# DeltaNet triangular inversion: the updates of T and of its transpose on 32 of 64 columns

## The chip, the cores and the metric

One core of a Trainium2 chip runs the whole kernel. The time is device microseconds from the start to the end of one execution. Before the change three executions took 1493.34, 1498.42 and 1501.33 us, so the median is 1498.42 us.

## The reference

The reference is a two-layer diffusion backbone with 256 context and 256 latent tokens of width 1024. The part that matters here is the gated DeltaNet of the even layer. It has 8 heads of size 64 in two directions, and the tokens are cut into chunks of 64:

```python
lower = jnp.eye(C) + bc[..., :, None] * jnp.einsum('bnhid,bnhjd->bnhij', kc, kc) * jnp.exp(jnp.where(strict, diff, -jnp.inf))
u0 = lax.linalg.triangular_solve(lower, bc[..., None] * vc, left_side=True, lower=True, unit_diagonal=True)
wk = lax.linalg.triangular_solve(lower, (bc * jnp.exp(g))[..., None] * kc, left_side=True, lower=True, unit_diagonal=True)
```

`lower` is a unit triangular 64 x 64 matrix for each chunk, head and direction: 8 x 8 x 2 = 128 of them. The kernel inverts them and then multiplies by the inverse. All of it is fp32.

## The kernel before, in words

`stage_delta_solve` does this. The 8 chunks are taken in `NP` = 4 pairs (`ORDER`), and `l` = 0, 1 is the chunk within a pair. For one chunk the 16 matrices lie as 8 indices `r` (0 to 3 forward, 4 to 7 backward) by two halves of the partitions (0 to 63 and 64 to 127), so one tile is 128 partitions x 512 elements. The inversion doubles blocks. After `begin` (L2450), which inverts blocks of 2, each of `LV` = 5 levels joins blocks of size b = 2, 4, 8, 16 and 32. Two copies are kept: T in `Tm` (T_mat) and its transpose in `d.TT` (inv_T). One level of one chunk is

- GpSimd, `joints` (L2395): the part of the matrix that joins the blocks, by a mask, into `Om` (O_T);
- TensorE, L2252: 16 products `Om` x `Tm` of 64 x 64 by 64 columns into the bank `XY(l)`;
- ScalarE, L2350: the bank to `Xm` (X_mat);
- TensorE, L2266: 16 products `Xm` x `TT` into the bank `YT(l)`, and, except at the last level, L2268: 16 products `TT` x `Xm` into `XY(l)`, alternately with those of L2266;
- VectorE, L2521 and L2522: `Tm` minus `XY(l)`, then `TT` minus `YT(l)`, each over 128 x 512.

The order on each engine is the order of the loops. TensorE runs, for each level, the L2252 products of both chunks, then products of the modulation weights (`mods`, L425, which belong to another part of the kernel), then L2266 and L2268 of chunk 0, a filler, L2266 and L2268 of chunk 1, and a filler. The fillers prepare the next pair (`spread` L835, `gram` L2164, `keys_values` L2180, `turn` L2194) or are pieces of the recurrence of a pair that is done (`ks` L2200 and L2205, `w_` L2211, `ds` L2219 and L2222). VectorE runs the two differences of a chunk first, and then the work of the same slot: `differences`, `matrices` (L2446 and L2447), `begin` (L2454, L2455, L2457) and `values` (L2464) of the next pair, or the recurrence's `residue`, `update` and `advance`. Semaphores tie the engines together: L2252 of a level waits for the difference of L2522 of the same chunk (`up_done`, L2250), the second `spread` waits for `matrices` (`gm_done`), and the second `keys_values` waits for `values` (`vc_done`). An fp32 product appears in the trace as two weight loads and two matmuls, so the 16 products of one line and one chunk are 32 records.

Of the kernel before, what the change touches and what calls it, by code (L numbers as in the profile page):

```python
# [13 lines left out]
ALU = mybir.AluOpType  # L14
# [19 lines left out]
DNC = 64  # L34
# [1935 lines left out]
def bc(ap, shape):  # L1970
    return ap.to_broadcast(shape)
# [75 lines left out]
def stage_delta_solve(k, d, qkvT, zT, of, ob, hi, lo, row, upto):  # L2047
# [21 lines left out]
    with ExitStack() as st:  # L2069
# [4 lines left out]
        AT, Tm, Om, Xm = d.AT, d.Tm, d.Om, d.Xm  # L2074
# [6 lines left out]
        XY, YT = (lambda l: k.pb[l]), (lambda l: k.pb[2 + l])  # L2081
# [6 lines left out]
        def v8(x):  # L2088
            return x.rearrange("p (r i) -> p r i", r=8)
# [13 lines left out]
        def pair_of(s):  # L2103
            return ORDER.index(s) // 2

        def event(pi, lv, l):
            return (pi * LV + lv) * 2 + l

        def inverted(s):
            return event(pair_of(s), LV - 1, ORDER.index(s) % 2) + 1  # L2110

        def mask(lv):
            return bc(d.lev[:, lv, :, :].rearrange("p d (o i) -> p d o i", o=1), [P, 2, 4, DNC])

# [27 lines left out]
        def _(pe):  # L2142
# [98 lines left out]
            for pi in range(NP):  # L2241
                for lv in range(LV):
                    it = pi * LV + lv
                    for l in range(2):
                        e = event(pi, lv, l)
                        pe.wait_ge(om_done.sem, om_done.at(e + 1))
                        if lv == 0:
                            pe.wait_ge(t2c_done.sem, t2c_done.at(2 * pi + l + 1))
                        if e >= 2:
                            pe.wait_ge(up_done.sem, up_done.at(e - 1))  # L2250
                        for r, q in each():
                            mm = pe.matmul(XY(l)[q, r * DNC:r * DNC + DNC], Om[q, l, r, :], Tm[q, (2 * pi + l) % 4, r, :], start=True, stop=True)  # L2252
                        mm.then_inc(x_done.sem, 1)
                    for m in mods[it]:
                        mod_products(k, pe, m)
                    if it == 12:
                        mod_turn(k, pe, mod_batch(4))
                    for l in range(2):
                        e = event(pi, lv, l)
                        un = ORDER[2 * pi + l]  # L2260
                        pe.wait_ge(xc_done.sem, xc_done.at(e + 1))
                        if e < 2:
                            pe.wait_ge(kc_done.sem, kc_done.at(e + 1))
                            pe.wait_ge(vc_done.sem, vc_done.at(e + 1))
                        for r, q in each():
                            mm = pe.matmul(YT(l)[q, r * DNC:r * DNC + DNC], Xm[q, l, r, :], d.TT[q, un, r, :], start=True, stop=True)  # L2266
                            if lv < LV - 1:
                                mm = pe.matmul(XY(l)[q, r * DNC:r * DNC + DNC], d.TT[q, un, r, :], Xm[q, l, r, :], start=True, stop=True)  # L2268
                        mm.then_inc(y_done.sem, 1)
                        if (pi, lv, l) in scan:  # L2270
                            piece(*scan[pi, lv, l])
                        if pi < NP - 1:
                            j = 2 * pi + 2
                            if (lv, l) == (0, 0):
                                spread(j)
                            if (lv, l) == (0, 1):
                                gram(j)
                            if (lv, l) == (1, 1):
                                spread(j + 1)
                            if (lv, l) == (2, 0):  # L2280
                                gram(j + 1)
                            if (lv, l) == (3, 0):
                                keys_values(j)
                            if (lv, l) == (3, 1):
                                keys_values(j + 1)
                            if (lv, l) == (4, 0):
                                turn(j)
                            if (lv, l) == (4, 1):
                                turn(j + 1)
                        else:  # L2290
                            if (lv, l) == (1, 0):
                                o.pe_sums(pe)
                            if (lv, l) == (2, 1):
                                o.pe_spread(pe, 0)
                            if (lv, l) == (3, 1):
                                o.pe_spread(pe, 1)
# [130 lines left out]
        def _(dve):  # L2427
# [82 lines left out]
            for pi in range(NP):  # L2510
                more = pi < NP - 1
                for lv in range(LV):
# [3 lines left out]
                    for l in range(2):  # L2516
                        e = event(pi, lv, l)
                        un = ORDER[2 * pi + l]
                        dve.wait_ge(y_done.sem, y_done.at(e + 1))
                        if lv < LV - 1:  # L2520
                            dve.tensor_tensor(Tm[:, (2 * pi + l) % 4, :, :], Tm[:, (2 * pi + l) % 4, :, :], v8(XY(l)[:, :]), ALU.subtract)  # L2521
                        dve.tensor_tensor(d.TT[:, un, :, :], d.TT[:, un, :, :], v8(YT(l)[:, :]), ALU.subtract).then_inc(up_done.sem, 1)  # L2522
                        if (pi, lv, l) in scan:
                            piece(*scan[pi, lv, l])
                        if more:
# [1154 lines left out]
```

## Time and profile before

The profiled execution took 1496.61 us, 1.81 us less than the median. Its span from the first to the last instruction is 1494.8 us.

| | before |
|---|---|
| median of three executions | 1498.42 us |
| the profiled execution | 1496.61 us |
| its span | 1494.8 us |
| mean granted TensorE clock | 0.976 |
| TensorE busy, matmuls / weight loads | 94% / 80% |
| VectorE / ScalarE / GpSimd busy | 61% / 44% / 13% |
| HBM read | 169.26 MB |

Each matmul has a weight load (PEld) and a matmul (PE) record. The matmuls are pipelined, so the duration of one says little, and the distance between the starts of consecutive records says how fast the engine goes. "Idle before" is the time that the engine stood still just before a group, followed by what released it. "issue" is idle time for which the profile shows no wait.

### The profile page before, as it was taken

The page shows a single profiled execution, that of the slowest core. Times are in us where ns is not written, and L with a number is a line of the kernel's source. Part 1 is how long each engine was busy: PE and PEld are TensorE (multiplying, and loading weights), DVE is VectorE, ACT ScalarE, POOL GpSimd, SP SyncE. Part 2 cuts the span into 40 slices and gives each one's busy share as a digit, 9 for nine tenths or more (in the row PEclk, how much of TensorE's full clock was granted, in tenths as well). Part 3 has the DMA queues.
Part 4 walks back from the last instruction along what each step waited for, and adds up shares of the span by engine and source line. Part 5 has one row for each costly group of instructions (what it writes and reads, how often), then busy time and mean ns, then how long its engine had stood idle before and what let it go on. Part 6 is the DMA issues. An engine that isn't in the chain of part 4 may idle for free. (4 is left out here: it accounts for less than half of the span.)

```text
span 1494.8 us, 30877 instructions
## 1 busy us (share of the span) xinstructions
PE 1403.3 (94%) x13473; PEld 1190.5 (80%) x13473; DVE 917.9 (61%) x1307; ACT 654.6 (44%) x1106; POOL 200.6 (13%) x168
## 2 busy tenths in 40 slices
PE   6888999899999999999999999989999999899998
PEld 3656676778887789878888888867878679899998
DVE  4477553555464666777765215788775786788844
ACT  4235525221231245666433115444452885555534
POOL 1000000233242031556100003000001100000000
PEclk9999989799999999999999999999999999999999
DMA  9321110153325234766432232222233005466553
GB/s 343 113 62 51 57 57 14 59 171 116 116 88 143 61 111 141 225 197 197 113 103 94 87 111 92 72 85 85 83 116 113 2 29 170 113 176 191 173 167 112
DMA packets 166096, 172.29 MB, mean 115 GB/s; under 512 B 7014, under 2 KB 131786, under 8 KB 165962
## 3 DMA queue, kind: packets, MB, share of 16 engines
q1 hardware_dynamic: 155120, 148.36, 32.6%
q10 hardware_dynamic: 9754, 17.77, 3.7%
q0 software_dynamic: 1088, 4.19, 0.8%
q8 instruction: 106, 1.74, 0.5%
q14 instruction: 28, 0.23, 0.1%
HBM read 169.26 MB, written 1.05 MB: 114 GB/s over the span
## 5 line engine op out<-in xcount | busy, mean ns | idle before, releaser
L806 PE MATMUL bank<-h,w_hi 128*128 128x256 f32 (+1 forms) x952 | 327.3, 344 | 2.9 <-issue 2.9
L810 PE MATMUL bank<-h,w_lo 128*128 128x256 f32 (+1 forms) x952 | 320.0, 336 | 0.0
L809 PE MATMUL bank<-h,w_hi 128*128 128x256 f32 (+1 forms) x952 | 319.7, 336 | 0.0
L336 DVE TENSOR_TENSOR w_lo<-w_raw,w_hi 128x2048 fp32r<-128x2048 f32 (+1 forms) x91 | 209.8, 2307 | 157.5 <-ACT w_hi L296 157.3
L296 ACT ACTIVATE w_hi<-w_raw 128x2048 fp32r<-128x2048 f32 x93 | 176.2, 1897 | 143.8 <-PE bank L806 139.7
L824 DVE SCALAR_TENSOR_TENSOR acc<-bank,params,acc 128x510 f32<-128x510 f32 (+3 forms) x272 | 173.1, 645 | 89.0 <-ACT acc L1867 61.5
L806 PEld LDWEIGHTS bank<-h,w_hi 128*128 128x128 f32 x952 | 181.9, 191 | 24.1 <-issue 6.1
L809 PEld LDWEIGHTS bank<-h,w_hi 128*128 128x128 f32 x952 | 182.0, 191 | 20.7 <-issue 2.9
L810 PEld LDWEIGHTS bank<-h,w_lo 128*128 128x128 f32 x952 | 181.6, 191 | 18.8
L1867 ACT ACTIVATE acc<-bank,params 128x512 f32<-128x512 f32 (+1 forms) x88 | 48.8, 580 | 153.8 <-DVE ffn_g_lo L1888 49.8
L2395 POOL TENSOR_TENSOR O_T<-A_T,dn_consts 128x512 f32<-128x512 f32 x40 | 52.4, 1317 | 314.4 <-DVE inv_T L2457 189.2
L806 PE MATMUL bank<-h_hi,w_hi_hyb 128*128 128x512 f32 (+1 forms) x184 | 78.0, 424 | 8.4 <-DVE dn_qkv L824 3.9
L2266 PEld LDWEIGHTS bank<-inv_T,X_mat 64*64 64x64 f32 x1280 | 67.6, 133 | 20.3 <-issue 10.5
L2266 PE MATMUL bank<-inv_T,X_mat 64*64 64x64 f32 x1280 | 72.4, 220 | 3.2 <-issue 3.2
L477 POOL TENSOR_TENSOR mod_sums<-mod_sums,mod_products 128x1024 f32<-128x1024 f32 x24 | 63.3, 2636 | 83.6 <-ACT mod_products L457 82.9
L2521 DVE TENSOR_TENSOR T_mat<-T_mat,bank 128x512 f32<-128x512 f32 x32 | 21.9, 683 | 85.5 <-PE bank L2268 85.5
L810 PE MATMUL bank<-h_hi,w_lo_hyb 128*128 128x512 f32 (+1 forms) x184 | 73.6, 400 | 0.0
L809 PE MATMUL bank<-h_lo,w_hi_hyb 128*128 128x512 f32 (+1 forms) x184 | 73.6, 400 | 0.0
L2268 PE MATMUL bank<-X_mat,inv_T 64*64 64x64 f32 x1024 | 62.6, 218 | 1.7 <-issue 1.7
L2268 PEld LDWEIGHTS bank<-X_mat,inv_T 64*64 64x64 f32 x1024 | 59.6, 135 | 0.0
L806 PE MATMUL bank<-ffn_g_hi,w_hi 128*128 128x256 f32 x176 | 50.7, 288 | 2.0 <-issue 2.0
L806 PEld LDWEIGHTS bank<-h_hi,w_hi_hyb 128*128 128x128 f32 (+1 forms) x184 | 35.2, 191 | 21.5 <-issue 10.0
(435 smaller groups left out, 2980.9 us busy)
## 6 DMA issues: line engine op xcount, KB each, us to landing
w_raw<-in_ffn_up SPq DMA_DIRECT2D x86, 512.0 KB, 5.2
w_raw<-in_mod_w SPq DMA_DIRECT2D x24, 1024.0 KB, 5.3
w_raw<-in_ffn_down SPq DMA_DIRECT2D x22, 1024.0 KB, 5.0
w_raw<-in_ssm_w_in SPq DMA_DIRECT2D x20, 1024.0 KB, 5.3
mod_late<-in_mod_w ACTq DMA_DIRECT2D x16, 1024.0 KB, 5.2
w_raw<-in_hyb_w_in SPq DMA_DIRECT2D x9, 1024.0 KB, 5.3
w_raw<-in_ssm_w_out SPq DMA_DIRECT2D x8, 1024.0 KB, 4.9
mod_early<-in_mod_w SPq DMA_DIRECT2D x4, 1024.0 KB, 14.6
```

Of the source, the lines that this page charges most:

```text
L296: act.activation(hi, raw, ACT.Copy).then_inc(k.hi_done.sem, 1)
L336: dve.tensor_tensor(lo, raw, hi.bitcast(F32), ALU.subtract).then_inc(k.lo_done.sem, 1)
L477: pool.tensor_tensor(acc, acc, k.modtmp[:, (3 * i + step - 1) % 2, :, :], ALU.add).then_inc(k.mod_added.sem, 1)
L806: mm = pe.matmul(out, wh, xh, start=(start and n == 0), stop=False)
L809: pe.matmul(out, wh, xl, start=False, stop=False)
L810: mm = pe.matmul(out, wl, xh, start=False, stop=(stop and n == last))
L824: ins = dve.scalar_tensor_tensor(out=ao, in0=bo, scalar=w(j), in1=ao, op0=ALU.mult, op1=ALU.add)
L1867: act.activation(acc[:, i % 4, :], self.bank(i), ACT.Copy, scale=self.taps(i)(1)).then_inc(self.seed_done.sem, 1)
L2266: mm = pe.matmul(YT(l)[q, r * DNC:r * DNC + DNC], Xm[q, l, r, :], d.TT[q, un, r, :], start=True, stop=True)
L2268: mm = pe.matmul(XY(l)[q, r * DNC:r * DNC + DNC], d.TT[q, un, r, :], Xm[q, l, r, :], start=True, stop=True)
L2395: pool.tensor_tensor(v24(Om[:, l, :, :]), v24(at(2 * pi + l)), mask(lv + 1), ALU.mult).then_inc(om_done.sem, 1)
L2521: dve.tensor_tensor(Tm[:, (2 * pi + l) % 4, :, :], Tm[:, (2 * pi + l) % 4, :, :], v8(XY(l)[:, :]), ALU.subtract)
```

## The change

At the level that joins blocks of size b, only the half of the columns that pairs one block with the other can change: T in one half of each 2b columns, and its transpose in the other half. The backward matrices swap the halves. The change streams and subtracts only these 32 of each 64 columns. The weights (stationary operands) of the products stay 64 x 64, and the number of products, instructions, semaphores and waits is the same. The moving operand becomes a strided view with runs of b elements, each bank holds 256 packed elements in place of 512, and the differences read and write `Tm` and `TT` in runs of b elements. L2252, the copy of L2350 and the mask of L2395 are as they were.

```diff
+        def half_columns(x, lv, other):
+            b = 2 << lv
+            shift = b if other else 0
+            return bass.AP(x.tensor, x.offset + shift, [x.ap[0], [4 * DNC + b - 2 * shift, 2], [2 * b, 2 * DNC // b], [1, b]])
+
+        def half_row(x, lv, r, other):
+            b = 2 << lv
+            return x.rearrange("p (n s b) -> p n s b", s=2, b=b)[:, :, int(other != (r >= 4)), :]
+
+        def half_bank(x, lv):
+            return x[:, 0:4 * DNC].rearrange("p (d n b) -> p d n b", d=2, b=2 << lv)
@@ TensorE
                         for r, q in each():
-                            mm = pe.matmul(YT(l)[q, r * DNC:r * DNC + DNC], Xm[q, l, r, :], d.TT[q, un, r, :], start=True, stop=True)
+                            h = slice(r * DNC // 2, r * DNC // 2 + DNC // 2)
+                            mm = pe.matmul(YT(l)[q, h], Xm[q, l, r, :], half_row(d.TT[q, un, r, :], lv, r, True), start=True, stop=True)
                             if lv < LV - 1:
-                                mm = pe.matmul(XY(l)[q, r * DNC:r * DNC + DNC], d.TT[q, un, r, :], Xm[q, l, r, :], start=True, stop=True)
+                                mm = pe.matmul(XY(l)[q, h], d.TT[q, un, r, :], half_row(Xm[q, l, r, :], lv, r, False), start=True, stop=True)
@@ VectorE
                         if lv < LV - 1:
-                            dve.tensor_tensor(Tm[:, (2 * pi + l) % 4, :, :], Tm[:, (2 * pi + l) % 4, :, :], v8(XY(l)[:, :]), ALU.subtract)
-                        dve.tensor_tensor(d.TT[:, un, :, :], d.TT[:, un, :, :], v8(YT(l)[:, :]), ALU.subtract).then_inc(up_done.sem, 1)
+                            th = half_columns(Tm[:, (2 * pi + l) % 4, :, :], lv, False)
+                            dve.tensor_tensor(th, th, half_bank(XY(l), lv), ALU.subtract)
+                        ih = half_columns(d.TT[:, un, :, :], lv, True)
+                        dve.tensor_tensor(ih, ih, half_bank(YT(l), lv), ALU.subtract).then_inc(up_done.sem, 1)
```

## Rows read from the trace of the kernel before

**Rows 1.** The page: TensorE's total, and the granted clock in 40 slices.

```profile
PE 1403.3 (94%) x13473; PEld 1190.5 (80%) x13473; DVE 917.9 (61%) x1307; ACT 654.6 (44%) x1106; POOL 200.6 (13%) x168
PEclk9999989799999999999999999999999999999999
```

**Rows 2.** Stretch: length, busy PE, PEld, DVE, ACT, POOL (records), clock, DMA share, GB/s.

```profile
279.00:482.00 203.00, 189.27 (x5341) 164.83 (x5339) 100.22 (x168) 48.94 (x83) 65.71 (x60) 0.98 0.40 127
```

**Rows 3.** Groups by line, 279 to 482 us: count, busy us, mean ns, idle before.

```profile
L2266 PE MATMUL bank<-inv_T,X_mat 64*64 64x64 f32 x1280 | 72.4, 220 | 3.2 <-issue 3.2
L2268 PE MATMUL bank<-X_mat,inv_T 64*64 64x64 f32 x1024 | 62.6, 218 | 1.7 <-issue 1.7
L2522 DVE TENSOR_TENSOR inv_T<-inv_T,bank 128x512 f32<-128x512 f32 x40 | 27.2, 680 | 13.1 <-PE bank L2266 13.1
L2521 DVE TENSOR_TENSOR T_mat<-T_mat,bank 128x512 f32<-128x512 f32 x32 | 21.9, 683 | 85.5 <-PE bank L2268 85.5
```

**Rows 4.** Timeline of PE, one product block: start, us, line, operands, records.

```profile
392.49 0.34 PE L2266 MATMUL bank<-inv_T,X_mat 64*64 64x64 f32 x4
...
394.28 0.33 PE L2268 MATMUL bank<-X_mat,inv_T 64*64 64x64 f32 x4
394.40 1.15 PE L2219 MATMUL bank<-rho,kv_tok 64*64 64x64 f32 x32
```

**Rows 5.** Timeline, products with a moving operand of 4 and of 8 columns.

```profile
203.13 0.19 PEld L1025 LDWEIGHTS bank<-dn_selectors,dn_gate_rows 16*64 16x64 f32 x2
...
203.51 0.19 PEld L1025 LDWEIGHTS bank<-dn_selectors,dn_gate_rows 16*64 16x64 f32 x2
...
484.97 1.06 PE L502 MATMUL bank<-base_consts,mod_partial_sums 128*128 128x8 f32 x8
485.96 1.15 PE L2211 MATMUL bank<-rho,inv_T 64*64 64x64 f32 x32
```

**Rows 6.** Waits of PE, 279 to 482 us: total us, times, longest.

```profile
PE bank L2180 <- DVE kv_tok L2464: 2.9, 3, 1.1
PE bank L2252 <- DVE inv_T L2522: 1.1, 2, 0.5
PE bank L835 <- DVE A_T L2447: 0.8, 1, 0.8
PE bank L835 <- DVE T_mat L2643: 0.3, 1, 0.3
```

**Rows 7.** Timeline: differences of 512 and VectorE work of 256 elements; a wait of PE.

```profile
296.69 0.42 DVE L2446 TENSOR_TENSOR mq<-bank,decay 128x256 f32<-128x256 f32 x1
297.03 0.41 DVE L2447 TENSOR_TENSOR A_T<-bank,decay 128x256 f32<-128x256 f32 x1
...
308.06 0.69 DVE L2521 TENSOR_TENSOR T_mat<-T_mat,bank 128x512 f32<-128x512 f32 x1 [1.51 <-PE bank L2268]
308.67 0.68 DVE L2522 TENSOR_TENSOR inv_T<-inv_T,bank 128x512 f32<-128x512 f32 x1
...
309.50 0.30 PE L2252 MATMUL bank<-T_mat,O_T 64*64 64x64 f32 x3 [0.54 <-DVE inv_T L2522]
```

**Rows 8.** Stretches with granted clock (third figure from the end), columns as in Rows 2.

```profile
202.00:204.00 2.00, 2.00 (x47) 1.85 (x46) 0.00 (x0) 1.00 (x4) 0.00 (x0) 1.00 0.00 0
206.00:208.00 2.00, 2.00 (x34) 2.00 (x34) 0.00 (x0) 0.00 (x0) 0.00 (x0) 0.50 0.00 0
338.30:340.30 2.00, 2.00 (x44) 2.00 (x42) 0.82 (x2) 0.00 (x0) 0.00 (x0) 0.50 0.00 0
```

**Rows 9.** Timeline of PE: L2252 of both chunks at the full clock and at half.

```profile
290.31 2.08 PE L2252 MATMUL bank<-T_mat,O_T 64*64 64x64 f32 x64
...
338.83 3.31 PE L2252 MATMUL bank<-T_mat,O_T 64*64 64x64 f32 x63
```

**Rows 10.** Timeline of PE: idle before it for which no wait is shown.

```profile
337.12 0.62 PE L2211 MATMUL bank<-rho,inv_T 64*64 64x64 f32 x14 [2.15 <-issue]
...
399.30 0.21 PE L2268 MATMUL bank<-X_mat,inv_T 64*64 64x64 f32 x1 [1.70 <-issue]
```

## Prediction, made before the changed kernel ran

> **What bounds the kernel now.** I read the page first. TensorE is busy in 94% of the span and no other engine is near that [rows 1], so time is won only where TensorE's own stream gets shorter. Then I read the stretch in which the inversion runs, 279 to 482 us. In its 203.00 us TensorE is busy for 189.27 us and VectorE for 100.22 us [rows 2]. VectorE has slack on the whole, and its part of the change counts only where TensorE stands still for it. The third view is the groups by line. The products that the change touches are 1280 + 1024 = 2304 records with 72.4 + 62.6 = 135.0 us of busy time, although L2266 and L2268 alternate and overlap, and the differences are 40 + 32 = 72 instructions of about 0.68 us [rows 3]. The fourth view is the list of what TensorE waited for, because only these waits can pass a gain of VectorE on to the end.
>
> **TensorE's products.** The busy time of overlapping records is no price, so I take the distance between starts. A product block of one chunk runs from 392.49 to 394.40 us, which is 1.91 us for 64 records, or 29.8 ns each [rows 4]. The change halves the columns that stream. Whether that shortens the block depends on what sets the 29.8 ns: the 64 streamed columns or the 64 columns of weights that each record loads first. The trace has rows that keep the weights and take the stream away. L1025 and its neighbours load 64 columns of weights and stream only 4. From 203.13 to 203.51 us ten loads start (two, then eight single ones), which is 38 ns each, at the full clock [rows 5, 8]. The stream is a sixteenth of that of our products and the record is no faster. L502 loads 128 columns of weights and streams 8: eight records from 484.97 to 485.96 us, or 124 ns each [rows 5]. That is 62 ns for 64 columns, and the two halves of the partitions, which our products use in turn, make about 31 ns of it. Both rows say that the weight loads set the pace, and these stay. So I cost the halved stream at nothing, 0 us. The bounds are from the same rows. On the upper side 38 ns against 29.8 ns would be a loss, but L1025 does not alternate between halves of the partitions as our products do, so I exclude a loss from this term. On the lower side the record could become half as long, if the stream set the pace after all: 2304 x 29.8 / 2 = 34.3 us less. I take the upper end, 0, since the rows with short streams lie there.
>
> The Trainium skill speaks on the same point. Its page "TensorE: Matmul & The Clock Gate", section "Wait — 56ns, not 53.3ns?", says that the distance of two matmuls never falls below about 25 ns, however few columns stream. If that floor alone were left, my estimate by that page would be (29.8 - 25) x 2304 = 11.1 us less. The trace speaks against it here, since records with 4 columns stand 38 ns apart [rows 5].
>
> **VectorE's differences.** Two differences of 512 elements in a row start 0.61 us apart (308.06 and 308.67), and two instructions of 256 elements that also read a bank start 0.34 us apart (296.69 and 297.03) [rows 7]. So each difference gives back 0.27 us, and the pair of one chunk 0.54 us. Over 72 of them that is 19 us of VectorE, nearly all beside TensorE's work. No row of before has runs as short as 2 elements. The bounds are 0.34 us, as for long runs, and 0.61 us, as if nothing were halved. I take 0.34 us, because these rows have the same element count, type and source.
>
> What of it reaches TensorE is in the waits. TensorE waited three times for L2464 (2.9 us in all, longest 1.1), twice for L2522 (1.1 us, longest 0.5), once for L2447 (0.8 us) and once for L2643 (0.3 us) [rows 6]. In all seven the pair of differences, or one of them, stands ahead of the awaited instruction on VectorE with nothing idle between. The clearest is the wait at 309.50: L2521 starts at 308.06 when the block is done, L2522 at 308.67, and TensorE goes on at 309.50 after 0.54 us of idleness [rows 7]. The three waits for L2464 and the one for L2447 are longer than 0.54 us and give 0.54 us each, 2.2 us together. The two for L2522 have 1.1 us together and give all of it or nearly so, 1.1 us. That for L2643 gives its 0.3 us. The sum is 3.6 us less. What is late next is TensorE itself, with its weight loads. The lower bound of this gain is 0 (short runs cost like whole rows), the upper one is the sum of the four rows, 5.1 us.
>
> **TensorE's clock.** This is the term with another sign. From 202 to 208 us TensorE does nothing but records with 64 columns of weights and streams of 4 columns. It is busy in 2.00 of 2.00 us both times, but the clock is 1.00 in the first stretch and 0.50 (1.2 of 2.4 GHz) in the second [rows 8]. So the low level came although the engine was never idle, while it streamed little. The change makes 2304 records stream half as much. The inversion has a low stretch already at 338.30 to 340.30 us [rows 8], right after an idle time of 2.15 us at 337.12 [rows 10]. Another pause, 1.70 us at 399.30 us in the middle of a product block, has no low stretch behind it yet [rows 10]: around it the products of 64 columns run. With 32 columns these streams shrink too, and I expect the clock to fall there.
>
> The price comes from L2252, which runs in both states. 64 records take 2.08 us at the full clock and 63 take 3.31 us mostly at half, so 1.2 us more [rows 9]. If a block of products is caught as well, 64 records lose another 1.91 us [rows 4], which makes 3.1 us. One more low stretch then costs 1.2 to 3.1 us. I take the middle, 2.2 us, and one such stretch. The count is between none (0 us) and five, which are the four longer pauses of [rows 6] (three for L2464, one for L2447) and the one at 399.30.
>
> The Trainium skill, in "TensorE: Matmul & The Clock Gate", section "HAM oscillation — how this bites in real kernels", ties the low clock to gaps in which the engine is idle. By that rule alone this term would be 0. The trace disagrees in one place, where the clock fell with no idle time at all [rows 8].
>
> Instructions, semaphores, DMAs and their queues stay as they are, so the other terms are 0. The copy of L2350 and the mask of L2395 come no later than before.
>
> **The sum.** 0 - 3.6 + 2.2 = 1.4 us less. The profiled execution took 1496.61 us (span 1494.8 us and 1.8 us around it), so it would take 1495.2 us. It was 1.8 us faster than the median of the three runs, so my forecast for a median is 1497 us. A measurement of this kernel can tell about 0.5%, or 7.5 us, from no change, so this is no change.
>
> **The rivals.**
> *The stream sets the pace.* Then the products halve, and the sum is -34.3 - 3.6 + 2.2 = -35.7 us, or 1463 us. For it: the streamed and the loaded columns are both 64 in our records, so the rows of these records can't tell the two apart. Against it: the records with 4 and with 8 streamed columns [rows 5]. A part of the gain, half of it, would give 1480 us. Chance 0.11 for both.
> *The clock falls at all five pauses* and each time takes a block of products and the L2252 behind it along. That is 5 x 3.1 = 15.5 us, less 3.6 us, or +12 us: 1510 us, slower. For it: the low clock with a busy engine at 206 us [rows 8]. Against it: the modulation products and L2252, with full streams, stand between the blocks. It decides the sign from 3.6 us on, so from the second low stretch, and makes more than 7.5 us from the fourth. Chance 0.15.
> *The supply of instructions takes the gain.* TensorE stands still for 2.15 and 1.70 us with no wait shown [rows 10]. If it arrives earlier at such a place and only waits longer there, the 3.6 us go back: about 1499 us, or 1501 us with the clock term. Chance 0.14, within no change.
> *The change doesn't do what it says on VectorE*: short runs cost as much as whole rows. It then has 1501 us, also no change. Chance 0.05.
>
> **How the numbers follow.** My forecast itself, 1497 us, has 0.55. With the last two rivals, no change has 0.74. The first rival gives 0.11 for faster and the second 0.15 for slower. The range must leave out no more than 2 in 10: it leaves the first rival out (0.11) and the far end of the second, and takes in the bounds of the terms and the spread of the three runs (-5 to +3 us). It goes from 1488 to 1509 us.
>
> **What would show it.** If the weight loads set the pace, the product blocks in the changed trace stay at about 1.9 us for 64 records, although each matmul record is shorter. If the stream set it, they take about 1.0 us. Starts of L2521 and L2522 should stand 0.34 us apart, at all levels. The waits for L2464 should fall from 2.9 to about 1.3 us, that for L2522 from 1.1 us to almost nothing. The clock in 399 to 403 us should show 0.5 somewhere. Wrong would be: blocks clearly shorter than 1.9 us, or low stretches at three places or more that were at full clock before.

## The result, and the profile after

The changed kernel is slower by 0.4%. Its median is 1502.16 us (20 executions, 1494.77 to 1513.11), beside 1496.75 us (20 executions) for the kernel before. The ratio is 1.0038, with a 95% interval of 1.0024 to 1.0053, so the change costs 5.7 us, between 3.6 and 7.9. The forecast was 1.4 us less. Five executions of the kernels below ran with a lower granted clock and took 1568 to 1990 us, and all medians, means and ratios leave them out.

The profiled execution took 1500.1 us, 3.5 us more than that of before. First its page, the lines that answer to [rows 1]:

```profile
span 1498.3 us, 30877 instructions
PE 1407.8 (94%) x13473; PEld 1195.3 (80%) x13473; DVE 898.1 (60%) x1307; ACT 655.1 (44%) x1106; POOL 200.1 (13%) x168
PEclk9999989799999999999999999999999999999999
```

VectorE lost 20 us of busy time and TensorE gained 4.5 us. The clock in 40 slices is the same line as before and shows nothing, since a slice is 37 us long. The loss has to be looked for in shorter stretches. In the changed file L2252 is L2264, L2266 is L2279, L2268 is L2281, L2521 is L2535, L2522 is L2537, L2180 is L2192, L2464 is L2477 and L2447 is L2460. These are the groups by line of the changed kernel, 279 to 486 us, as in [rows 3]:

```profile
L2279 PE MATMUL bank<-inv_T,X_mat 64*64 64x32 f32 x1280 | 73.3, 223 | 6.1 <-issue 6.1
L2281 PE MATMUL bank<-X_mat,inv_T 64*64 64x32 f32 x1024 | 63.6, 221 | 1.5 <-issue 1.5
L2537 DVE TENSOR_TENSOR inv_T<-inv_T,bank 128x256 f32<-128x256 f32 x40 | 16.6, 415 | 20.2 <-PE bank L2279 20.1
L2535 DVE TENSOR_TENSOR T_mat<-T_mat,bank 128x256 f32<-128x256 f32 x32 | 13.4, 418 | 95.1 <-PE bank L2281 95.1
```

The products stream 32 columns and their mean record is 223 and 221 ns, as with 64 columns. Next, one product block of the changed kernel in the timeline of TensorE (start, us, line, operands, records), beside [rows 4]:

```profile
287.24 0.31 PE L2279 MATMUL bank<-inv_T,X_mat 64*64 64x32 f32 x4
...
289.01 0.30 PE L2281 MATMUL bank<-X_mat,inv_T 64*64 64x32 f32 x4
289.13 0.56 PE L2176 MATMUL bank<-dn_qkv 64*64 64x64 f32 x12
```

From 287.24 to 289.13 us it is 1.89 us for 64 records. The differences in the timeline of VectorE, beside [rows 7]:

```profile
286.28 0.42 DVE L2535 TENSOR_TENSOR T_mat<-T_mat,bank 128x256 f32<-128x256 f32 x1 [7.01 <-PE bank L2281]
286.62 0.41 DVE L2537 TENSOR_TENSOR inv_T<-inv_T,bank 128x256 f32<-128x256 f32 x1
```

They start 0.34 us apart. Of the 32 such pairs in the trace, with runs of 2 to 16 elements, 31 stand 0.33 to 0.34 us apart and one 0.28 us; before it is 0.59 to 0.61 us, and one 0.55 us. And what TensorE waited for in 279 to 482 us (total us, times, longest), beside [rows 6]:

```profile
PE bank L2279 <- issue: 6.1, 3, 3.8
PE bank L2264 <- issue: 2.0, 2, 1.2
PE bank L2281 <- issue: 1.5, 1, 1.5
PE bank L2192 <- DVE kv_tok L2477: 1.3, 2, 0.7
PE bank L835 <- issue: 0.8, 1, 0.8
PE bank L2223 <- issue: 0.5, 1, 0.5
PE bank L835 <- DVE A_T L2460: 0.3, 1, 0.3
```

The waits for VectorE fell from 5.1 us to 1.6 us, which is 3.5 us and nearly the 3.6 us that the forecast counted on. But the idle time with no wait shown is now 6.1 + 2.0 + 1.5 + 0.8 + 0.5 = 10.9 us. The same view of before has 3.2 us before L2266, 2.2 before L2211, 1.7 before L2268 and 1.6 before L2252, which is 8.7 us (8.6 us in a second profile of it). The last reading is the granted clock in stretches of 40 to 70 us (columns as in [rows 2]; the clock is the third figure from the end). First before, then after:

```profile
279.00:340.00 61.00, 56.42 (x1543) 48.73 (x1541) 27.97 (x48) 13.18 (x23) 18.21 (x17) 0.95 0.42 141
460.00:500.00 40.00, 36.52 (x835) 31.16 (x831) 18.73 (x30) 5.99 (x10) 7.66 (x8) 0.96 0.40 106
500.00:570.00 70.00, 67.29 (x583) 58.54 (x580) 46.06 (x72) 31.83 (x56) 13.12 (x18) 1.00 0.27 77
```

```profile
279.00:340.00 61.00, 57.90 (x1497) 50.16 (x1495) 20.37 (x47) 13.20 (x23) 18.05 (x16) 0.89 0.43 141
318.00:320.00 2.00, 2.00 (x43) 2.00 (x42) 1.97 (x4) 0.25 (x1) 0.00 (x0) 0.50 0.03 8
460.00:500.00 40.00, 36.16 (x825) 31.37 (x822) 13.96 (x27) 5.99 (x10) 7.82 (x9) 0.91 0.35 82
484.00:488.00 4.00, 4.00 (x69) 3.88 (x68) 2.32 (x5) 0.00 (x0) 0.00 (x0) 0.50 0.00 0
500.00:570.00 70.00, 67.82 (x602) 58.44 (x603) 44.76 (x67) 29.30 (x51) 13.15 (x18) 0.98 0.30 91
```

A stretch of length s at mean clock c holds 2 x (1 - c) x s of time at the half clock, because the clock is either 1 or 0.5. For before that is 61 x 0.10 + 40 x 0.08 + 0 = 9.3 us. For after it is 61 x 0.22 + 40 x 0.18 + 70 x 0.04 = 23.4 us. (Between 340 and 460 us the two kernels are alike.) One of the new low stretches begins in a product block:

```profile
317.01 0.25 PE L2279 MATMUL bank<-inv_T,X_mat 64*64 64x32 f32 x2 [2.00 <-issue]
...
319.42 2.79 PE L2264 MATMUL bank<-T_mat,O_T 64*64 64x64 f32 x62
```

TensorE stands still for 2.00 us, runs on, and soon after it is at 0.50; L2264 takes 2.79 us for 62 records where [rows 9] has 2.08 us for 64. So both findings of the profile are named: new idle time without a wait took the place of VectorE's, and the clock is low for longer. The experiments test both.

### The profile page after: what moved, and what is told of

Its sections match the earlier page's. It is cut to its first block and busy times, and to the rows that moved or that the text cites. A ratio compares the mean times of both kernels' runs of the same rounds, so it can differ in the third digit from the quotient of the medians.

```text
span 1498.3 us, 30877 instructions
## 1 busy us (share of the span) xinstructions
PE 1407.8 (94%) x13473; PEld 1195.3 (80%) x13473; DVE 898.1 (60%) x1307; ACT 655.1 (44%) x1106; POOL 200.1 (13%) x168
## 3 DMA queue, kind: packets, MB, share of 16 engines
q8 instruction: 106, 1.74, 0.5%
## 5 line engine op out<-in xcount | busy, mean ns | idle before, releaser
L2279 PEld LDWEIGHTS bank<-inv_T,X_mat 64*64 64x64 f32 x1280 | 67.1, 137 | 23.0 <-issue 13.4
L2279 PE MATMUL bank<-inv_T,X_mat 64*64 64x32 f32 x1280 | 73.3, 223 | 6.1 <-issue 6.1
L2535 DVE TENSOR_TENSOR T_mat<-T_mat,bank 128x256 f32<-128x256 f32 x32 | 13.4, 418 | 95.1 <-PE bank L2281 95.1
L2281 PE MATMUL bank<-X_mat,inv_T 64*64 64x32 f32 x1024 | 63.6, 221 | 1.5 <-issue 1.5
L2281 PEld LDWEIGHTS bank<-X_mat,inv_T 64*64 64x64 f32 x1024 | 58.2, 137 | 0.0
```

The costliest lines, as they stand in the source:

```text
L2279: mm = pe.matmul(YT(l)[q, h], Xm[q, l, r, :], half_row(d.TT[q, un, r, :], lv, r, True), start=True, stop=True)
L2281: mm = pe.matmul(XY(l)[q, h], d.TT[q, un, r, :], half_row(Xm[q, l, r, :], lv, r, False), start=True, stop=True)
```

## The experiments

"Half-clock time" below is 2 x (1 - mean granted clock) x span, as a mean over the executions of a kernel. It covers the whole execution. In the kernel before it is about 70 us, most of it outside the inversion.

**The two halves of the change, each alone.** The first kernel has only VectorE's half:

```diff
-                            h = slice(r * DNC // 2, r * DNC // 2 + DNC // 2)
-                            mm = pe.matmul(YT(l)[q, h], Xm[q, l, r, :], half_row(d.TT[q, un, r, :], lv, r, True), start=True, stop=True)
+                            h = slice(r * DNC, r * DNC + DNC)
+                            mm = pe.matmul(YT(l)[q, h], Xm[q, l, r, :], d.TT[q, un, r, :], start=True, stop=True)
...
-                        dve.tensor_tensor(ih, ih, half_bank(YT(l), lv), ALU.subtract).then_inc(up_done.sem, 1)
+                        dve.tensor_tensor(ih, ih, half_columns(v8(YT(l)[:, :]), lv, True), ALU.subtract).then_inc(up_done.sem, 1)
```

(The product into `XY(l)` and the difference of `Tm` likewise.)

> The products stream all 64 columns again and only the differences take 32 columns (they read the wanted half of each bank in place). If the loss of the change comes from TensorE's clock because less is streamed (my theory), this version keeps the 3.6 us that the shorter differences give back and none of the loss: about 1493 us, ratio to before 0.997 to 0.998, and stretches at half clock within 300 to 500 us only where the kernel before has them. If the loss comes from the strided short runs of the differences, or only from the moved order of events, it is still there: ratio 1.003 or more.

Measured: 1497.3 us (12 executions) beside 1495.8, a ratio of 1.0003 (0.9991 to 1.0015). Half-clock time 70.3 us, before 69.8 us. So there is no clock loss, and the expected gain of 3.6 us did not come either. What TensorE waited for in this kernel, 279 to 482 us:

```profile
PE bank L2279 <- issue: 6.2, 2, 3.7
PE bank L2264 <- issue: 2.1, 2, 1.3
PE bank L2281 <- issue: 1.7, 1, 1.7
PE bank L2192 <- DVE kv_tok L2477: 1.3, 2, 0.8
PE bank L2223 <- issue: 1.2, 1, 1.2
PE bank L835 <- DVE A_T L2460: 0.3, 1, 0.3
```

The waits for VectorE are 1.6 us here too, 3.5 us below before. The idle time without a wait is 11.2 us in place of 8.7. It gives most of the gain back. The second kernel has only TensorE's half. VectorE gets its old work back, and some more, as an extra instruction beside each difference:

```diff
                             th = half_columns(Tm[:, (2 * pi + l) % 4, :, :], lv, False)
+                            tr = half_columns(Tm[:, (2 * pi + l) % 4, :, :], lv, True)
+                            dve.tensor_tensor(tr, tr, tr, ALU.max)
                             dve.tensor_tensor(th, th, half_bank(XY(l), lv), ALU.subtract)
```

(The same for `d.TT`.)

> The products stream 32 columns, as in the change, but VectorE does as much as before: each difference of 256 elements has a second instruction of 256 elements beside it (a maximum of the other half with itself, which changes nothing). Clock theory: the loss without the gain, so before plus 5.4 plus 3.6 us, about 1506 us, ratio 1.006, and low-clock stretches as in the changed kernel. Rival (the differences cause the loss): no loss, ratio 1.000. Rival (the stream sets the pace and something else hides it): below 1.000.

Measured: 1503.1 us (6 executions), ratio 1.0044 (1.0027 to 1.0061), which is +6.6 us. Half-clock time 90.1 us. The loss is there without VectorE's gain, so it comes with the short streams. As a price of the streams alone the figure is rough: VectorE is busy for 108.2 us in 279 to 482 us here and for 100.2 us before, and TensorE waits for it for 9.5 us instead of 5.1. A cleaner pair follows with the fourth kernel.

**A dose.** The third kernel streams 8 columns in the same products:

```diff
-                            h = slice(r * DNC // 2, r * DNC // 2 + DNC // 2)
-                            mm = pe.matmul(YT(l)[q, h], Xm[q, l, r, :], half_row(d.TT[q, un, r, :], lv, r, True), start=True, stop=True)
+                            h = slice(r * DNC // 2, r * DNC // 2 + 8)
+                            mm = pe.matmul(YT(l)[q, h], Xm[q, l, r, :], d.TT[q, un, r, 0:8], start=True, stop=True)
```

> The changed kernel with products that stream 8 columns instead of 32; so most of the updates is left out and the output is not the reference's. TensorE does the same number of products with the same weight loads and a quarter of the streaming. Clock theory: much slower, at least 10 us over the changed kernel, up to 50 us, with half-clock stretches in most rounds of the inversion; where the clock is full the blocks of 64 records stay at 1.9 us. If the stream sets the pace of the blocks it is faster than before by 30 us or more. If streaming matters for neither, it equals the changed kernel within 0.3%.

Measured: 1513.87 us (3 executions), ratio 1.0124 (1.0102 to 1.0146), which is +18.5 us. Half-clock time 131.1 us. The fourth kernel is the change once more, beside these three.

> The changed kernel once more, for a second profile on the same chip as the three others. Clock theory: ratio 1.004, and in this profile again more half-clock time between 300 and 500 us than in before (6.8 us there), at places that follow a pause beside the products of 32 columns, but not the same ones. If the low stretches of the first profile were chance, this one has as many as before and the cause is open.

Measured: 1502.57 us (7 executions), ratio 1.0041 (1.0025 to 1.0056); half-clock time 94.3 us. Against the first kernel the differences are the same size and only the products stream 32 columns instead of 64 (and pack their results): by the means that is 5.8 us more, give or take 2.4. In 300 to 500 us the clock is 0.93 in this profile and 0.98 before. The stretches show where the low clock lies. First streams of 64 columns with half differences, then the change again, then streams of 8:

```profile
279.00:340.00 61.00, 57.00 (x1550) 48.80 (x1547) 21.10 (x46) 13.79 (x24) 19.60 (x18) 0.96 0.43 141
```

```profile
279.00:340.00 61.00, 58.41 (x1461) 51.03 (x1459) 19.76 (x45) 13.30 (x23) 18.13 (x17) 0.86 0.42 140
460.00:500.00 40.00, 36.16 (x744) 30.61 (x742) 11.85 (x22) 7.35 (x13) 9.51 (x10) 0.83 0.35 81
```

```profile
400.00:460.00 60.00, 56.04 (x1582) 52.07 (x1578) 28.12 (x56) 15.53 (x26) 17.47 (x17) 0.91 0.27 91
```

With 8 columns even 400 to 460 us, where the kernels with streams of 64 and of 32 columns above stand at 1.00, falls to 0.91. The four kernels ran beside each other, so their means can be set against their half-clock time:

| products stream | mean time | half-clock time | us per us of half clock, against the first |
|---|---|---|---|
| 64 columns (first kernel) | 1496.7 us | 70.3 us | |
| 32, full work on VectorE (second) | 1502.9 us | 90.1 us | 6.2 / 19.8 = 0.31 |
| 32, the change (fourth) | 1502.5 us | 94.3 us | 5.8 / 24.0 = 0.24 |
| 8 columns (third) | 1514.8 us | 131.1 us | 18.1 / 60.8 = 0.30 |

The fewer columns stream, the longer the clock is low, and each such microsecond costs 0.24 to 0.31 us. It can't cost more than 0.5, as work at half speed for 1 us is 0.5 us of work left over, and part of the time TensorE idles. The 20 executions of the changed kernel, which all do the same work, say the same without any comparison of kernels. The one with the least half-clock time (71.7 us) took 1494.77 us, the one with the most (114.9 us) took 1513.11 us, and a line through all 20 rises by 0.39 us per us (correlation 0.95). The four with less than 75 us took 1494.8 to 1497.1 us, as does the kernel before (median 1496.75 us).

**What sets the pace of a product block.** Two kernels take the kernel before and cut the weights to 32 columns, one with streams of 64 columns, one with 32:

```diff
-                            mm = pe.matmul(YT(l)[q, r * DNC:r * DNC + DNC], Xm[q, l, r, :], d.TT[q, un, r, :], start=True, stop=True)
+                            few = slice(q.start, q.start + DNC // 2)
+                            mm = pe.matmul(YT(l)[few, r * DNC:r * DNC + 64], Xm[q, l, r, 0:DNC // 2], d.TT[q, un, r, 0:64], start=True, stop=True)
```

> The kernel before with products of the updates that load 32 columns of weights instead of 64 and stream 64; the other half of each result is left out, so the output is not the reference's. If the weight loads alone set the pace, as predicted, a block of 64 records falls from 1.9 to about 1.0 us and the kernel is faster by up to 33 us, unless instructions can't be supplied so fast. If the stream holds the pace just as much (64 columns each, side by side), the block stays at 1.9 us and the time is that of before, ratio 1.000.

> As the run before, but the products stream 32 columns too; again part of the work is left out. Both limits of the block are halved. If loads and streams are the two limits, a block of 64 records takes about 1.0 us and the kernel could save 33 us less what the clock takes. If the supply of instructions is the limit behind them, TensorE's idle time without a shown wait, about 9 us in before, grows by tens of us and at most 10 us are saved.

Weights of 32 and streams of 64 columns: 1494.95 us, ratio 0.9993 (0.9976 to 1.001). Both at 32: 1488.14 us, ratio 0.9949 (0.9923 to 0.9975). The starts of groups of 4 records, first the one, then the other, then the kernel with streams of 8 columns and full weights:

```profile
300.76 0.30 PE L2267 MATMUL bank<-inv_T,X_mat 64*32 64x64 f32 x4
...
300.99 0.30 PE L2267 MATMUL bank<-inv_T,X_mat 64*32 64x64 f32 x4
```

```profile
292.04 0.25 PE L2267 MATMUL bank<-inv_T,X_mat 64*32 64x32 f32 x4
...
293.43 0.25 PE L2267 MATMUL bank<-inv_T,X_mat 64*32 64x32 f32 x4
```

```profile
284.85 0.28 PE L2279 MATMUL bank<-inv_T,X_mat 64*64 64x8 f32 x4
...
285.08 0.28 PE L2279 MATMUL bank<-inv_T,X_mat 64*64 64x8 f32 x4
```

Weights 32, stream 64 is 0.23 us for 8 records, or 29 ns each. Weights 64, stream 8 is also 0.23 us for 8. Both at 32 is 1.39 us from 292.04 to 293.43 for 88 records, or 15.8 ns each. So the loads and the stream are two limits of equal height, and to remove one leaves the other. The Trainium skill's "TensorE: Matmul & The Clock Gate", section "Wait — 56ns, not 53.3ns?", states a floor of about 25 ns between the starts of two matmuls. The trace shows 15.8 ns here, in a stream of records that alternates between the two halves of the partitions. Within one half that is 31.6 ns on the mean.

With both at 32, the product blocks should save 2304 x (29.8 - 15.8) ns = 32 us, and the execution gains 7.6 us. TensorE's idle time without a wait grew from 8.7 to 16.3 us there, and the waits for VectorE from 5.1 to 6.4 us. Half-clock time went from 68.3 to 80.7 us. At 0.3 us per us that is an estimated 4 us. With the longer idle times and the 7.6 us gained, about 20 of the 32 us are accounted for; where the rest went is open. The forecast that the idle time would grow by tens of us was too high.

**The differences as small as can be.** If VectorE were still in the way, differences of next to nothing would help. This is the first kernel with differences of 16 elements:

```diff
-                        dve.tensor_tensor(ih, ih, half_columns(v8(YT(l)[:, :]), lv, True), ALU.subtract).then_inc(up_done.sem, 1)
+                        dve.tensor_tensor(d.TT[:, un, 0, 0:16], d.TT[:, un, 0, 0:16], YT(l)[:, 0:16], ALU.subtract).then_inc(up_done.sem, 1)
```

> The kernel of the first experiment (streams of 64) with each difference cut to 16 elements, so the updates are left out nearly whole. VectorE's share of every wait of TensorE is gone: about 0.55 us more for each of the waits that were left. If gains of VectorE reach the end, this is 3 us or more faster than before, ratio 0.998 or less. If the supply of instructions takes them, as I now think, the time stays within 1.5 us of before, and TensorE's pauses before its records number 2614, 3122, 4013, 4776, 6174 and 6937 (counted from its first) add up to more than the 12.5 us of the first experiment.

Measured: 1495.51 us, ratio 0.9992 (0.9977 to 1.0007). What TensorE waited for, 279 to 482 us:

```profile
PE bank L2279 <- issue: 6.3, 3, 4.1
PE bank L2264 <- issue: 2.6, 3, 1.4
PE bank L2223 <- issue: 2.3, 1, 2.3
PE bank L2281 <- issue: 1.4, 1, 1.4
PE bank L2192 <- DVE kv_tok L2477: 0.7, 1, 0.7
```

VectorE holds TensorE up for 0.7 us in all, and there is no gain. The idle time without a wait is 12.6 us. VectorE's waits and this idle time together are 13.8 us before, 12.8 with half differences and 13.3 with tiny ones. So most of what VectorE no longer holds up comes back as idle time without a wait. The kernel before was profiled once more beside it.

> The kernel before once more, for a second profile. If the pauses without a shown wait are the supply of instructions, they stand before the same records of TensorE as in the first profile (3122, 4776, 6174, 6937) whatever the time of day in the run; there is none, or a short one, before 2614 and 4013, where TensorE has just waited for VectorE. Low-clock stretches between 300 and 500 us: about 7 us in all.

One execution took 1498.1 us. The four pauses stand before the same records as in the first profile. Two more came, before 4013 (0.9 us) and 4394 (1.1 us), so which of the places show a pause varies from one execution to the next, and where they are does not.

**Where the pauses without a wait come from.** Every pause has one of a few places in the count of TensorE's 13473 matmul records. I list the number of records before each pause of over 0.6 us for which no wait stands (in brackets the us from start to start), from 309 to 482 us:

| kernel | pauses |
|---|---|
| before | 3122 (2.4), 4776 (1.9), 6174 (1.5), 6937 (3.4) |
| before again | 3122 (1.3), 4013 (0.9), 4394 (1.1), 4776 (1.7), 6174 (1.3), 6937 (3.7) |
| after | 2614 (2.2), 3122 (0.8), 4013 (1.1), 4394 (1.1), 4776 (1.7), 6174 (1.4), 6937 (4.1) |
| differences alone | 2614 (2.7), 3122 (1.4), 4013 (1.1), 4776 (2.0), 6174 (1.5), 6937 (3.9) |
| tiny differences | 2486 (0.8), 2614 (1.9), 3122 (2.5), 4013 (1.6), 4776 (1.6), 6174 (1.2), 6937 (4.3) |

The distances are multiples of 127, give or take a record or two: 3122 - 2614 = 508 = 4 x 127, 4013 - 3122 = 891 = 7 x 127, 4776 - 4394 = 382 = 3 x 127, 6174 - 4776 = 1398 = 11 x 127, 6937 - 6174 = 763 = 6 x 127. The page of before has 106 packets of 16.4 KB on the DMA queue "q8 instruction" (1.74 MB). In the kernel before, one of them is under way in 334 to 338 us, where TensorE pauses with no wait, and in the kernel with half differences one is in 311 to 316 us:

```profile
q8 instruction: 1, 0.02, 1.8%
```

```profile
q8 instruction: 1, 0.02, 1.2%
```

The pause in the timeline of the latter:

```profile
315.15 0.37 PE L2279 MATMUL bank<-inv_T,X_mat 64*64 64x64 f32 x2 [2.52 <-issue]
```

The page after has the same 106 packets. 13473 records by 106 packets are 127.1 records a packet, the step of the table. That reads as an engine whose next packet of instructions is late, and the times of the packets in the traces bear it out. I take the two profiles of before, the two of the change, and those of the kernels with half differences, with streams alone, with tiny differences and with the 32 added records below. In 279 to 486 us they have 47 pauses of TensorE of over 0.4 us with no wait shown, and every one ends 1.23 to 1.56 us after a packet of this queue has ended. In before the packets end at 335.88, 397.84, 444.98 and 478.86 us, and TensorE goes on at 337.12, 399.30, 446.40 and 480.29 us. The 33 pauses with a wait end at any distance from a packet (0.04 to 6.81 us), and none of them in that range. It can be tested by an edit, too: insert records and see whether the pauses move with the program or stay at their count.

```diff
             turn(1)
+            for r, q in each():
+                pe.matmul(O[q, r * DNC:r * DNC + DNC], d.TT[q, ORDER[0], r, :], k.ident[q, q], start=True, stop=True)
             for pi in range(NP):
```

> The kernel before with 16 more products (32 records of TensorE, 0.9 us) at the start of the inversion, into a bank that nobody reads then. It shows what the pauses without a shown wait hang on. Supply of instructions: they stay at the same count of records from the start of the program (3122, 4776, 6174, 6937), so 32 records earlier in the work. Anything tied to the work (a missing record of a wait, a bank, a buffer): they come 32 records later in the count (3154, 4808, 6206, 6969). The waits for VectorE (2129, 2433, 2633, 3729, 3937, 5545 in before) move by 32 in either case.

These are 32 records more. Five of the six pauses with a wait moved by exactly 32: 2129, 2433, 2633, 3937 and 5545 became 2161, 2465, 2665, 3969 and 5577. The sixth, 3729, should stand at 3761. There is none; a pause of the other kind stands two records ahead of it, at 3759, with no wait shown, and covers it. (30 of the 64 records of L2254, L2252 before, come ahead of it and 34 behind it, so it lies two records before the second chunk.)

```profile
357.32 1.27 PE L2254 MATMUL bank<-T_mat,O_T 64*64 64x64 f32 x34 [0.88 <-issue]
```

It ends 1.27 us after a packet, and 3759 is 4013 - 2 x 127. The other pauses without a wait stand at 2486, 3249, 4267, 4904, 6174, 6937 and 7065, and none at 3154, 4808, 6206 or 6969. Two of the four expected numbers stayed (6174 and 6937). The other two are gone, and pauses stand one step further on: 3249 is 3122 + 127, 4904 is 4776 + 128. So the pauses belong to the count of instructions and not to a piece of work. Their lengths change, too: 0.8 us at 3249, where the profile of before has 2.4 us at 3122. The one execution took 1493.95 us with more work in it. One execution against a spread of several microseconds says nothing on the time.

**Can the clock be kept up with wider streams?** In [rows 8] it falls at 206 us, behind products that stream 4 columns (L1025 and its neighbours). One kernel repeats their moving operand 16 times, so they stream 64 columns, and takes them in an order that alternates between the two halves of the output's partitions (before, five products in a row write one half; the operands lie on 16 partitions throughout). A second one has this order with 4 columns as before:

```diff
-                for n in range(NCH):
-                    tok = slice(n * DNC, n * DNC + DNC)
+                def wide(o, row, n, pick):
                     for par in range(2):
-                        r = slice(par * HD, par * HD + HD)
+                        many = bc(d.colsel[0:16, pick + par, :].rearrange("p (o i) -> p o i", o=1), [16, 16, 4])
+                        pe.matmul(B_BANK[par * HD:par * HD + HD, o:o + 64].rearrange("p (o i) -> p o i", i=4),
+                                  d.rows[0:16, row, n * DNC:n * DNC + DNC], many, start=True, stop=True)
...
+                for first in (0, 64):
+                    for n in range(NCH):
                         for dr in range(2):
+                            wide(first + n * 8 + dr * 4, (0, 3)[dr] if first == 0 else 2, n, 2 * dr)
+                for n in range(NCH):
+                    wide(128 + 4 * n, 1, n, 2)
```

> The kernel before, with one edit elsewhere, in the attention stage: the 80 small products of L1025 to L1027 stream their 4 columns 16 times over, so 64 columns each, with the same weight loads (the surplus lands in columns that a later product overwrites, so the result is the same). Clock theory with the sign turned round: more streaming on the same loads costs nothing and keeps the clock, so the 10 to 14 us at half clock after 205 us are gone, TensorE gets back a third to a half of that, 3 to 6 us, ratio 0.997 or less. If streaming has no bearing on the clock: the low stretch stays and the ratio is 1.000. If streams cost time: above 1.000.

> The control for the run before: the same 80 products in the same new order (which alternates between the two column halves of the array at each product), with 4 columns each. Clock theory: the low stretch after 205 us stays at 10 us or more; the order alone gives at most 160 records x (38 - 29) ns = 1.4 us, ratio 0.999 to 1.000. If it was the order, this one is as fast as the run before.

Measured: 64 columns 1492.6 us, ratio 0.9979 (0.9968 to 0.9991); 4 columns in the new order 1490.3 us, ratio 0.9961 (0.9949 to 0.9973). Half-clock times 64.7 and 60.7 us, before 69.2 us. The stretches, first with 64 columns, then with 4:

```profile
206.00:208.00 2.00, 2.00 (x42) 2.00 (x41) 0.00 (x0) 0.00 (x0) 0.00 (x0) 0.50 0.00 0
```

```profile
204.00:206.00 2.00, 2.00 (x72) 2.00 (x72) 0.00 (x0) 0.80 (x4) 0.00 (x0) 1.00 0.03 8
208.00:210.00 2.00, 2.00 (x42) 2.00 (x41) 0.00 (x0) 0.00 (x0) 0.00 (x0) 0.50 0.00 0
```

Wider streams did not keep the clock up here: it falls as before. The expected ratio of 0.997 was nearly met, but not by the streams, since the order alone gives more. Against it the 64 columns cost 2.7 us by the means, give or take 1.8, and their half-clock time is no lower. 72 records in 2 us are 28 ns each, where L1025 in the order of before needs 38 ns [rows 5] and more: 160 records less 10 ns each are 1.6 us. The 8.5 us less of half clock, at 0.24 to 0.31 us each, are an estimated 2.0 to 2.6 us. That leaves about 2 of the 5.8 us (4.0 to 7.6) without a cause shown. A last kernel joins half differences (first kernel) and the 64-column streams.

> The edit of run 9 together with the halved differences of run 1 (streams of 64 columns in the inversion). The first experiment gave nothing by itself because the pauses took it, so this should be as fast as run 9, within 1 us, and faster than before and than the change: ratio 0.997 or less.

It took 1490.82 us, ratio 0.9966 (0.9955 to 0.9978), with 63.2 us of half clock. Against the 64-column streams alone the mean is 1.8 us lower, from 5 and 10 executions and with an uncertainty as large (1.7 us), so whether the differences add anything here is open. The kernel that only reorders the products of L1025 has the lowest ratio of those that compute the whole reference, 0.9961, and it does not have the change.

## Why the prediction was wrong, point by point

**The products cost nothing less.** This held: the block takes 1.89 us against a forecast of about 1.9 us, and the rival by which the stream sets the pace (1463 us) is out. The reason was half right. "The weight loads set the pace" is true of the changed kernel. In the kernel before, loads and streams are equal limits (29 ns with either one cut, 15.8 ns with both). The rows with short streams could show only that the loads are a limit, not that they are the only one.

**The differences on VectorE.** The local part held to the figure: starts 0.34 us apart at all levels that have both differences, waits for VectorE down by 3.5 us against 3.6 us predicted, those for L2464 from 2.9 to 1.3 us, that for L2522 to nothing.

**The differences at the end of the kernel.** The failed step is "What is late next is TensorE itself, with its weight loads". What is late next is the supply of instructions: all 47 pauses without a wait end 1.23 to 1.56 us after a packet of instructions, and the idle time without a wait grew from 8.7 to 11.2 us when 3.5 us of waits went. The kernel with half differences alone gained nothing (1.0003), nor did that with tiny ones (0.9992). The interval of the first reaches from a gain of 1.3 to a loss of 2.2 us, so 3.6 us are excluded. This was the third rival, with a chance of 0.14, and its mechanism is the one that holds: TensorE gets there sooner and waits longer. It was in view already in [rows 10], with 2.15 and 1.70 us. The rival asked what these pauses do with an earlier arrival, and the sum did not: it counted the 3.6 us in full, with no term for them.

**The clock.** The sign held, and so did the mechanism in so far as shorter streams go with more half-clock time, but the term was mis-sized: +2.2 us predicted. Short streams measured +6.6 us (4.0 to 9.1) with full work on VectorE, and 5.8 us between the first and the fourth kernel. In the profiled execution there are new or longer low stretches at 318, 335, 484 and 556 us. At full clock before were those of 318 and 556 us and the first half of the one at 335 us (335 to 338), so the forecast's own sign of being wrong (three places or more) is just met. These are more stretches of it, with that of 399 us among them:

```profile
335.00:341.00 6.00, 5.48 (x103) 5.29 (x102) 2.55 (x5) 1.05 (x2) 0.00 (x0) 0.50 0.40 148
399.00:403.00 4.00, 2.49 (x87) 2.43 (x85) 1.27 (x4) 0.00 (x0) 0.00 (x0) 1.00 0.41 147
556.00:560.00 4.00, 3.34 (x18) 3.09 (x20) 3.02 (x7) 1.61 (x4) 2.45 (x3) 0.57 0.00 0
```

In the kernel before the first of them is at 0.77 and the last at 1.00. In the other profile of the change the stretches 279 to 340 and 460 to 500 us are lower still (0.86 and 0.83). Two assumptions in the sum made it small. One was the count: "I expect the clock to fall there", at one pause, 399.30 us. The clock is 1.00 in 399 to 403 us in the changed kernel, and it fell at other places. The other was the place: the term looked only at pauses in the middle of the inversion, while the stretch at 481 us was already low in the kernel before and only grew, and the one at 556 us lies behind the inversion. The gap between the two kernels with streams of 64 and of 32 columns is 20 to 24 us of half clock at 0.24 to 0.31 us each.

The second rival had this mechanism, with five pauses and 15.5 us. The measured cost lies between my term and it.

The Trainium skill's "TensorE: Matmul & The Clock Gate", section "HAM oscillation — how this bites in real kernels", ties the low clock to idle gaps. The runs here show that gaps are not all. TensorE's idle time in 279 to 486 us (waits and no waits together) is 12.8 us with half differences and streams of 64 columns, where the half-clock time is 70.3 us, and 12.4 us in the second profile of the change, where it is 94.3 us. (The idle time is that of the profiled execution, the half-clock time the mean of all.) The idle time does not tell the two kernels apart, and what was changed between them is the streamed columns.

**The sum.** 0 - 3.6 + 2.2 = -1.4 us was forecast. With the measured terms it is 0 (products), about 0 (differences, given back to the supply) and 5.8 to 6.6 (clock). That is +5.8 to +6.6 us, and 5.7 us was measured (3.6 to 7.9).

**What stays open.** Why the clock fell at 318 and 556 us and not at 399 us; why streams of 64 columns that use 16 of 128 partitions did not keep it up at 206 us; and how the 5.8 us of the new order split. That the pauses end with the arrival of packets is shown by their count and by the times of the packets. What makes a packet late is not shown, and there is no run in which the supply was made faster.

## What to carry to other kernels

Ask of every idle time without a wait what it does when its engine arrives earlier, and do so before a gain from removed waits is counted: here 3.5 us of waits turned into time at the next late packet of instructions. When a change only shortens the streams of products whose weights stay, it can win nothing if the loads are an equal limit, and it can lose by the granted clock, so look first at the half-clock time of the kernel, in stretches shorter than the 40 slices. Two kernels that each do one half of a change show such a pair of effects at once.

## What the runs showed of the hardware

- Of an fp32 product of 64 x 64 by 64 columns, the weight load and the stream are equally long limits: 29 ns for a record with the weights cut to 32 columns or the stream to 8, 15.8 ns with both at 32.
- Pauses of 0.4 to 4 us with no wait shown stand at a few counts of TensorE records, whatever the work there. Their distances are multiples of about 127 records, and the 13473 records by the 106 packets of instructions are 127.1. All 47 pauses of over 0.4 us in eight profiles end 1.23 to 1.56 us after such a packet. 32 added records moved pauses with a wait by 32 and none of those without.
- The same number of products with shorter streams, on the same weights, has more time at the half clock: 70, 90 to 94 and 131 us with 64, 32 and 8 columns. Each such us costs 0.24 to 0.31 us between kernels, and 0.39 us among the 20 executions of the changed one.
- Small products (16 x 64 by 4 columns) that alternate between the halves of the output's partitions run at 28 ns a record, and in the order of before at 38 ns or more. The order alone made the kernel 5.8 us faster (0.9961).
